# Splitting the token gather of a mixture-of-experts kernel: 128 slots first, expert 0 between the pieces of the rest

## The reference, cut to what matters

```python
h = rmsnorm(x, norm_ffn_g[i]) * (1.0 + sc_f) + sh_f
...
for e in range(N_EXPERTS):
    he = jax.nn.silu(t @ w_gate[e]) * (t @ w_up[e])
    y = y + combine[:, e, None] * (he @ w_down[e])
```

## Time and profile before

| | |
|---|---|
| median of 3 executions | 760.78 us |
| the profiled execution: its own time | 762.43 us |
| its span, first to last instruction | 760.7 us |
| PE busy | 712.6 us, 94% |
| DVE busy | 232.6 us, 31% |
| ACT busy | 164.8 us, 22% |
| POOL busy | 39.7 us, 5% |
| read from HBM | 273 MB, 360 GB/s over the span |
| granted clock of PE, mean | 0.996 of full speed |

### The profile page before, as it was taken

How to read it: one execution, slowest core, us unless ns; L and a number is a source line. 1 busy time by engine, 2 the same in 40 slices (tenths; PEclk the granted TensorE clock), 3 DMA queues, 4 the chain that set the end, 5 groups by cost and what they waited for, 6 DMA issues and landing times.

```text
span 760.7 us, 12156 instructions
## 1 busy us (share of the span) xinstructions
PE 712.6 (94%) x4474; PEld 408.1 (54%) x4474; DVE 232.6 (31%) x640; ACT 164.8 (22%) x378; POOL 39.7 (5%) x71
## 2 busy tenths in 40 slices
PE   4798899999889999989999999999999998999995
PEld 1444455554454545437877877655555554455542
DVE  1025533222211212143674862373322221121213
ACT  4014431111101111142323322253111110111113
POOL 0000011110000000000000000000000000000000
PEclk9999999999999999999999999999999999999999
DMA  8999999999999999999588539583999999999951
GB/s 356 409 416 411 414 419 411 417 416 419 415 419 414 417 417 417 415 395 373 243 291 341 199 111 394 198 348 131 411 394 417 416 418 416 417 416 416 414 238 57
DMA packets 61234, 274.90 MB, mean 361 GB/s; under 512 B 4481, under 2 KB 17921, under 8 KB 39553
## 3 DMA queue, kind: packets, MB, share of 16 engines
q1 hardware_dynamic: 61184, 274.23, 89.8%
HBM read 273.17 MB, written 1.05 MB: 360 GB/s over the span
## 4 chain that ended last, share of the span: by engine, by line
PE 80%; DMA 14%; SPq 2%; DVE 2%; ACT 1%; issue 1%; DVEq 0%; ACTq 0%
PE bank L533 71%; DMA ring<-in_exp_w_up_dram 8%; PE bank L688 4%; DMA ring<-in_ada_w_dram 3%; DMA reg_a<-in_band_dram 3%; PE bank L675 2%; SPq L392 1%; PE bank L802 1%; PE bank L1009 1%; DVE ye L1502 0%; SPq L389 0%; ACT reg_h L1148 0%; DVE reg_a L1505 0%; PE bank L663 0%; PE bank L927 0%
## 5 line engine op out<-in xcount | busy, mean ns | idle before, releaser
L533 PE MATMUL bank<-ring,xe 128*64 128x256 f32 x1984 | 229.5, 384 | 10.8 <-DMA ring<-in_exp_w_up_dram 9.2
L533 PEld LDWEIGHTS bank<-ring,xe 128*64 128x64 f32 x1984 | 141.6, 137 | 82.4 <-issue 15.5
L533 PE MATMUL bank<-ring,heT 128*64 128x512 f32 x512 | 123.9, 604 | 0.0
L1502 DVE TENSOR_TENSOR reg_c<-reg_c,bank 128x128 f32<-128x128 f32 x64 | 18.5, 288 | 271.9 <-ACT reg_c L1216 271.9
L505 POOL COPY xe<-reg_a 128x512 f32 x62 | 38.2, 617 | 666.5 <-PE bank L533 370.9
L1148 ACT ACTIVATE ye<-bank 128x512 f32<-128x512 f32 (+1 forms) x72 | 41.7, 585 | 139.4 <-PE bank L533 139.2
L1216 ACT ACTIVATE reg_c<-bank 128x128 f32<-128x128 f32 x64 | 17.8, 278 | 249.1 <-PE bank L533 246.3
L533 PE MATMUL bank<-reg_b,ring 128*128 128x256 f32 x256 | 58.2, 381 | 0.8 <-ACT reg_b L1360 0.8
L1502 DVE TENSOR_TENSOR reg_b<-bank,colp 128x512 f32 x64 | 44.3, 692 | 44.2 <-issue 36.8
L533 PEld LDWEIGHTS bank<-ring,heT 128*64 128x64 f32 x512 | 31.2, 136 | 47.2 <-issue 47.0
L533 PE MATMUL bank<-ring,cact 128*32 128x512 f32 (+1 forms) x320 | 36.1, 548 | 19.1 <-DMA ring<-in_ada_w_dram 17.2
(11 more groups left out here) (164 smaller groups left out, 513.7 us busy)
## 6 DMA issues: line engine op xcount, KB each, us to landing
ring<-in_exp_w_gate_dram SPq DMA_DIRECT2D x64, 1024.0 KB, 15.3
ring<-in_exp_w_up_dram SPq DMA_DIRECT2D x64, 1024.0 KB, 17.4
ring<-in_exp_w_down_dram SPq DMA_DIRECT2D x64, 1024.0 KB, 14.0
ring<-in_ada_w_dram SPq DMA_DIRECT2D x48, 1024.0 KB, 13.1
ring<-in_w_qkv_dram SPq DMA_DIRECT2D x12, 1024.0 KB, 13.1
ring<-in_w_o_dram SPq DMA_DIRECT2D x4, 768.0 KB, 5.6
x_sb<-in_x_dram SPq DMA_DIRECT2D x1, 1024.0 KB, 5.2
reg_a<-in_band_dram SPq DMA_DIRECT2D x1, 1024.0 KB, 19.8
```

Of the source, the lines that this page charges most:

```text
L533: return nc.tensor.matmul(o_, l_, r_, start=start, stop=stop)
L1502: return nc.vector.tensor_tensor(o_, a_, b_, op)
```

## The change

The gather is split. `first_gather` sorts only slots 0 to 127 (16 matmuls with 128 columns) into banks 1 to 3, in turn; then PE computes expert 0's hidden layer, which needs only those. The other 384 slots are gathered in three pieces: blocks 0 and 1, then the transpose of expert 0's hidden layer, block 2, then expert 0's down product, blocks 3 to 7. In layer 0 `columns(3)` now follows those, and `turn_weights` comes after it, in banks 4 and 5. Expert 1's own turn no longer has expert 0's down product.

ACT stores 8 blocks of 128 slots and later 8 blocks of 384, around expert 0's `silu` and `take_ye`, and loads its table for Silu before the first of them. DVE makes `pick` in eight instructions (128 columns for both token halves, then 384). `G_F` is made after expert 0 has left DVE, and each part of the overflow list comes one expert later. POOL's wait before expert 1's tokens is for the last of 16 stored blocks. SP's program is not touched.

```diff
-            def gather(L):
...
+            def gather_of(dst, kk, c0, c1):
+
+                for t in range(T):
+                    last = mm(dst, h_str[:, t, kk, :], pick[:, t, c0:c1], t == 0, t == T - 1)
+                last.then_inc(S("gathered"), 1)
+
+            def first_gather(L):
...
+                pe.wait_ge(S("pick_ready"), 2 * T * L + T)
+                for kk in range(KC):
+                    if kk >= 3:
+                        pe.wait_ge(S("hS_ready"), 2 * KC * L + kk - 2)
+                    gather_of(bank[1 + kk % 3][:, 0:P], kk, 0, P)
+
+            def gather(L, k0, k1):
+
+                if k0 == 0:
+                    pe.wait_ge(S("pick_ready"), 2 * T * L + 2 * T)
...
+                for kk in range(k0, k1):
+                    if kk >= 4:
+                        pe.wait_ge(S("hS_ready"), 2 * KC * L + KC + kk - 3)
+                    gather_of(bank[4 + kk % 4][:, 0:NSLOT - P], kk, P, NSLOT)
...
-            def first_hidden(L):
+            def first_expert(L):
...
+                first_gather(L)
                 pe.wait_ge(S("ring_first", s), fill)
                 pe.wait_ge(S("ring_mid", s), fill)
...
                 last.then_inc(S("gu_ready", L), 1)
+                gather(L, 0, 2)
+                turn_he_of(L, 0, 0)
+                gather(L, 2, 3)
+                down_of(L, 0, s, fill, 0)
+                gather(L, 3, KC)
+                if L == 0:
+                    columns(3)
                 turn_weights(L)
-                turn_he_of(L, 0, 0)
...
                 hidden_of(L, e, *loaded(L, e), e)
-                down_of(L, 0, *loaded(L, 0), 0)
                 turn_he_of(L, e, e)
...
             def expert_at(L, e):
                 silu(L, e, e % 2, exp_at(L, e)[0])
                 if e == 0:
+                    evac_gather(L, 0, 3)
+                    take_ye(L, 0, 0, exp_at(L, 0)[0])
+                    evac_gather(L, 3, KC)
                     evac_weights(L)
-                else:
+                elif e >= 2:
                     take_ye(L, e - 1, 1 - e % 2, exp_at(L, e - 1)[0])
...
-            for e in range(FRONT):
+            expert_at(0, 0)
+            dve.wait_ge(S("cols_full"), 4)
+            column(0, G_F, cols_at(3))
+            for e in range(1, FRONT):
                 expert_at(0, e)
-                overflow_list(0, e)
+                overflow_list(0, e - 1)
```

More of the change, by code:

```diff
@@ L351, in cols_at @@
             if n == 3:
-                return bank[4][:, 0:KC]
+                return bank[3][:, 0:KC]
             if n == 4:
@@ L637, in route @@
                     keep_busy(3, 6)
-            def gather(L):
+            def gather_of(dst, kk, c0, c1):
[3 more added lines that the diff above has]
+            def first_gather(L):
                 pe.wait_ge(S("xr_ready"), 4 * L + 4)
                 pe.wait_ge(S("x_kept"), 4 * L + 4)
[L643 to L655, removed]
+                pe.wait_ge(S("pick_ready"), 2 * T * L + T)
[6 more added lines that the diff above has]
+                    pe.wait_ge(S("pick_ready"), 2 * T * L + 2 * T)
+                    pe.wait_ge(S("strided_ready"), L + 1)
+                    if L == 0:
+                        pe.wait_ge(S("acc_act"), 4)
+                for kk in range(k0, k1):
+                    if kk >= 4:
+                        pe.wait_ge(S("hS_ready"), 2 * KC * L + KC + kk - 3)
+                    gather_of(bank[4 + kk % 4][:, 0:NSLOT - P], kk, P, NSLOT)
             def turn_weights(L):
@@ L660, in turn_weights @@
                 for b in range(2):
+                    pe.wait_ge(S("hS_ready"), 2 * KC * L + KC + 5 + b)
                     for s in range(2):
                         for t in range(T):
-                            last = nc.tensor.transpose(bank[6 + b][:, s * SEQ + t * P:s * SEQ + (t + 1) * P],
+                            last = nc.tensor.transpose(bank[4 + b][:, s * SEQ + t * P:s * SEQ + (t + 1) * P],
                                                        pickw[:, t, (2 * b + s) * P:(2 * b + s + 1) * P], ident)
@@ L917, in _ @@
             route(0)
-            gather(0)
             for e in range(FRONT):
@@ L1138, in _ @@
             route(1)
-            gather(1)
             for e in range(FRONT):
@@ L1208, in evac_weights @@
                     act.wait_ge(S("pwT_full"), L * 2 + b + 1)
-                    copy(pwT[:, 2 * b:2 * b + 2, :], bank[6 + b][:, :].rearrange("p (s q) -> p s q", s=2))\
+                    copy(pwT[:, 2 * b:2 * b + 2, :], bank[4 + b][:, :].rearrange("p (s q) -> p s q", s=2))\
                         .then_inc(S("pwT_ready"), 1)
@@ L1480, in _ @@
             route(1)
-            evac_gather(1)
+            evac_first(1)
             for e in range(FRONT):
@@ L1647, in route, with is_slot @@
                 dve.wait_ge(S("x_back"), 4 * L + 4)
-                for t in range(T):
-                    then(nc.vector.tensor_scalar(pick[:, t, :], iota, slot_of[0][:, t, :], None, ALU.is_equal))
-                    stt(pick[:, t, :], iota, slot_of[1][:, t, :], pick[:, t, :], ALU.is_equal, ALU.add)\
-                        .then_inc(S("pick_ready"), 1)
+                def is_slot(t, i, c0, c1):
+                    dst, numbers, slot = pick[:, t, c0:c1], iota[:, c0:c1], slot_of[i][:, t, :]
+                    if i == 0:
+                        return nc.vector.tensor_scalar(dst, numbers, slot, None, ALU.is_equal)
+                    return stt(dst, numbers, slot, dst, ALU.is_equal, ALU.add)
+                for t in range(T):
+                    last = is_slot(t, 0, 0, P)
+                then(last)
+                for t in range(T):
+                    is_slot(t, 1, 0, P).then_inc(S("pick_ready"), 1)
+                for t in range(T):
+                    then(is_slot(t, 0, P, NSLOT))
+                    is_slot(t, 1, P, NSLOT).then_inc(S("pick_ready"), 1)
                 dve.wait_ge(S("gexp"), L * 2 + 2)
@@ L1948, in _ @@
             route(1)
-            for e in range(FRONT):
+            expert_at(1, 0)
+            for e in range(1, FRONT):
                 expert_at(1, e)
-                overflow_list(1, e)
+                overflow_list(1, e - 1)
             later_experts(1)
```

34 lines of the change are left out of this document (19 added, 15 removed).

## The result

The changed kernel takes 768.49 us (median of 4 executions, 766.91 to 769.28). The kernel before, run beside it on the same chip, takes 761.49 us (4 executions, 760.22 to 762.94). The ratio is 1.0086, 95% interval 1.0065 to 1.0107: slower, and above the top of the predicted range (765.6 us). The profiled execution took 768.62 us with a span of 766.9 us; before it was 762.43 and 760.7 us. So 6.2 us of span are to be explained.

The account below looks back on a forecast made before the run. Each expert stage was taken to end a fixed stretch of PE work after expert 19's up matrix lands, so DMA loads bound it. From the median, 760.78 + 2.1 - 0.4 = 762.5 us; range 760.0 to 765.6 us.

Parts of the forecast that it names:

- The work of the split: Layer 0, PE: first piece 3.8 us, then expert 0's work and remaining columns; expert 4 issued at 105.95 us, not 99.87 us.
- bank waits: First gather piece: ACT emptying three banks could add up to 3 us; taken as nothing, 1 us kept for the range.
- new wait: Layer 1: expert 1 waits for the last gathered block to pass ACT (about 0.65 us) and POOL (0.61 us), starting at 526.95 us.
- 2.1 us lost: Layer 0: late issue puts expert 4's gate landing at 110.75 us, not 108.7 us, moving all later landings; bounds 1.7 and 3.7 us.
- the rule: Layer 0: expert 4 lands 4.8 us after issue or one MiB behind the former landing, whichever is later.
- 0.4 us gained: Layer 1: expert 6's down matrix lands at 543.3 us, not 543.7 us; ends -0.9 and +2.0 us.
- the landing still decides: Layer 1, expert 19: PE arrives at 639.2 us, the load's landing allows 640.9 us, so PE's delay does not count.
- The clock: Layer 1, expert 19: the profiled half-clock drop, 1.7 us, goes away, and none is expected in the changed kernel.
- B: Rival, clearly slower: slow bank emptying, expert 6's down matrix late, or one clock drop; 764.5 to 766.5 us, chance 0.24.
- A (faster): Rival: layer 1's early expert 5 load keeps its lead, if PE's delay stays under 1 us; 758.8 us, chance 0.14.
- C (nothing): Rival: queue not dry at 106 us, layer 0's loss under 1 us, both layers cancel; 761 us, chance 0.12.
- two signs: Prediction wrong if expert 4 is issued before 102 us, or layer 1's expert 19 comes over 2 us nearer its gather.

Follow-up runs that it names:

- pe_later: cols_first with three more 512-column matmuls on PE in layer 1 before expert 1's hidden layer; 765.78 us against 762.7 for the kernel before, ratio 1.0038.
- cols_first: The changed kernel with layer 0's `columns(3)` back ahead of the first gather piece; 764.12 us against 762.7 for the kernel before, ratio 1.0016.
- old_layer1: cols_first with layer 1's gather, order and banks as in the kernel before, only layer 0 split; 761.96 us against 762.7, ratio 0.9989.
- sp_wait_h1: The kernel before, with SP waiting for expert 1's hidden layer before issuing expert 4 in layer 0; 767.56 us, ratio 1.0062 to the kernel before.
- sp_wait_h0: The kernel before, with SP waiting for expert 0's hidden layer before issuing expert 4 in layer 0; 763.32 us against 762.65, ratio 1.0013.
- gu_first_split: cols_first with SP issuing the next expert's gate and up matrices ahead of this one's down matrix, from expert 5 on; 758.2 us against 762.65, ratio 0.9942.
- layer0_only: The changed kernel with layer 1 as in the kernel before, late `columns(3)` kept; 766.25 us against 761.88 for the kernel before, ratio 1.0064.
- pad_layer0: The kernel before with 16 unused four-column matmuls added on PE in layer 0 behind the weights' transposes; 767.67 us against 761.0, ratio 1.0077.
- pad_layer1: The kernel before with 16 unused four-column matmuls added on PE in layer 1 behind the weights' transposes; 767.04 us against 761.0, ratio 1.0067.

## Why the prediction was wrong, point by point

**The work of the split: right.** From the first piece to the issue of expert 4 it measured 107.11 - 86.63 = 20.48 us; the sum had 105.95 - 85.6 = 20.35. The first piece took 3.73 us (90.36 - 86.63; forecast 3.8, 0.117 us for each pass), and the bank waits did not show. In layer 1, behind the gather, expert 1 came after 21.70 us (forecast 526.95 - 505.4 = 21.55), expert 2 after 26.49 (26.4), expert 6's gate matrix was issued after 25.62 (25.5), its down matrix after 32.71 (32.6). The "new wait" is there, 0.72 us for POOL at expert 1. The Trainium skill (TensorE: Matmul & The Clock Gate, "LDWEIGHTS") gives the time to load a stationary operand by its columns alone, 107 ns for 128. The padding agrees, 3.49 us for 32 passes or 0.109 us each with four columns streamed, and the 0.117 us of the first piece lies near it.

**"2.1 us lost" in layer 0: the mechanism right, the term mis-sized, 4.3 us.** The step that failed is "expert 4's lands at 110.75 us, not 108.7 us". It compared landings, and took the queue to be full until the last one at 106.2 us. The DMA was down to 164 GB/s at 104 us, and five executions of four kernels put the loss at the issue less 102.8 us, 1.1 us more than the rule. The other 1.1 us is an issue at 107.11 us and not at 105.95: 0.75 us of it the half clock ahead of the gather, without which the same kernel issued at 106.36 us. The Trainium skill (DMA: Bandwidth & Descriptors, "Anatomy of one DMA") fits 2.0 us plus bytes/436e3 to single transfers that GpSimd issues; SP issues these, so the 4.4 us and the loss of 1.7 us that the prediction took from it were estimates for another path. The trace has 4.8 us for one MiB on an empty queue, and the measured loss went the other way.

**"0.4 us gained" in layer 1: wrong, 1.8 us lost.** Up to expert 6's down matrix the forecast held by the landings (0.7 us ahead). The step that failed is the next one, "PE arrives at expert 19 at 639.2 us, the landing allows 640.9 us, so the landing still decides". Both were compared at expert 19 alone. But the landings still hung on PE at expert 9's down matrix (561.29 us before), 18 us behind the landing at 543.3 us with which my sum ended: its issue follows expert 5's down product, and PE was 2.23 us later. The sign of it stood in the trace before: 262 GB/s at 561 to 563 us. The page's slices of 19 us hide it. The bytes moved since the gather's start show that the loss arises up to there, and not behind it. After 54 us, ahead of that issue, the six profiles whose layer 1 is that of before have 15.98 to 16.31 MB and the four with nothing but the split in layer 1 15.71 to 15.98 MB. After 62 us it is 18.97 to 19.16 against 18.17 MB, and after 130 us still 47.32 to 47.45 against 46.54 MB; 0.8 to 0.9 MB are 1.9 to 2.2 us at the loads' rate. Expert 19 says the same: in before's own profile, with its wait of 2.17 us, it came 135.73 us behind the gather, but in the five others with this layer 1 135.00 to 135.24 us, and with the split 137.18 to 137.53 us. So the 1.8 us of the ledger are a low figure, and 1.9 to 2.5 us a better one. *pe_later* shows the dependence directly, and so does the 2.16 us between cols_first and old_layer1.

**"The clock": partly right, partly missed.** That before's drop at expert 19 would go came true: 3.67 us behind 1.14 us. That no other would come did not: 1.65 us behind layer 0's combine, which was in no part of the sum. No row of the kernel before has a drop there, and I had no reason to ask what the longer code would do to the "issue" wait.

**The rivals.** The result lies above B's 764.5 to 766.5 us. B's direction was right, but its mechanisms did not come: there were no bank waits, expert 6's down matrix landed at the early end, and the drop of the clock came elsewhere. A (faster) fell for the reason given against it. Its condition, PE less than 1 us later, wasn't met (2.2 us). C (nothing) failed at once: the queue was dry at 106 us. Of the two signs that the prediction named for its being wrong, an issue before 102 us and an expert 19 over 2 us nearer to its gather, neither came: it missed on the side that these do not watch.

**What is shown and what isn't.** Shown by undoing or by doing alone: layer 0's loss is SP's issue time (*cols_first*, *sp_wait_h1*, and the profile of *sp_wait_h0*), layer 1's is PE's delay (*old_layer1*, *pe_later*, *gu_first_split*), and the drop between the layers came in *cols_first* without layer 0's loss and in *layer0_only* (4.45 us for the 24 matmuls) without layer 1's split. Open: why PE's "issue" wait behind the combine grows. All eight runs with the split layer 0, the first one included, have 2.86 to 2.99 us; kernels with PE's layer 0 as before have 1.90 to 1.98, 2.18 us with the padding in layer 1, 3.42 us with it in layer 0. The traces hold a strong hint. In all fourteen profiles exactly one transfer of the DMA queue that the profile calls "q8 instruction", 0.02 MB, stands in the 4.5 us ahead of the wait's end, and it begins 2.4 to 2.7 us before that end (337.1 us in before, 336.97 us in cols_first). In before six of the 24 matmuls, 1.06 us, still run ahead of the wait of 1.90 us, in cols_first none does, and 1.06 + 1.90 = 2.96 us is the wait there. So PE probably waits for instructions in both, and in the longer program it has none left a little sooner. No run tried that by itself, so it is not shown, and neither is why the clock then drops in seven of these eight and not in *old_layer1*.

## What to carry to other kernels

A load queue's slack has to be read from the rate in fine stretches, and not from landings: count the bytes that the stretches lack at full rate, and look at every place up to the point where PE first waits for a load, since each one that runs dry passes PE's delay on to all later loads. If a fill order can be chosen, put what the next step needs first ahead of what it needs last: here that was worth 1.0% (6.5 us by the landings, the rest a half clock that was gone), while the work put between the gather's pieces only moved a pause. A small matmul that one queue waits for belongs ahead of the long ones, even if nothing on its own engine needs it soon.

## What the runs showed of the hardware that was not expected

- A queue that is full to 416 GB/s falls to 164 GB/s some 2 us before its last transfer lands (104 to 105 us, landing 106.2 us), so a refill that meets the last landing is already over 3 us late (106.36 us, loss 3.50 us).
- TensorE's clock fell to half behind 3.5 us of four-column passes without any gap (granted 0.57 at 109 to 111 us in *pad_layer0*, 0.50 at 531 to 533 us in *pad_layer1*), in two kernels of two. The split gather's 128-column passes of the same length had no such drop behind them.
- The length of a wait does not decide the clock by itself: 2.86 us behind the combine left it at full speed in *old_layer1* and 2.96 us halved it in *cols_first*; 1.88 us in front of expert 19 was followed by half clock in *pad_layer0*, and 1.94 us behind the combine in *sp_wait_h0* was not.
